# Prompt heads of a hybrid decoder: score banks, value tiles, mask and the second gelu rearranged

## The reference

```python
def trunk_layer(x, pos, conv_prev, h0, lp, paged=None):
    z = rms_norm(x, lp['attn_norm']) @ lp['w_in']      # split in xr, cq, ckv, kpe, u, v, g
    y_rg, h_last, conv_new = rglru_branch(xr, conv_prev, h0, pos, ...)   # softplus(-lam), convolution of 4 taps, scan
    q = (rms_norm(cq, lp['q_a_norm']) @ lp['w_uq']).reshape(bsz, t, MLA_HEADS, QK_HEAD)
    q_nope = rms_norm(q[..., :QK_NOPE], lp['q_nope_norm'])
    q_pe = rope(rms_norm(q[..., QK_NOPE:], lp['q_rope_norm']), pos)
    latent, k_pe = rms_norm(ckv, lp['kv_a_norm']), rope(rms_norm(kpe, lp['k_rope_norm']), pos)
    y_at = mla_prompt(...) if paged is None else mla_sample(...)
    y_cm, v_rows = sgu_branch(jax.nn.gelu(u), jax.nn.gelu(v), ...)
    proj = jnp.einsum('btnc,ncd->btnd', jnp.stack([y_rg, y_at, y_cm], axis=2), lp['w_branch'])
    x = x + jnp.sum(jax.nn.sigmoid(g) * proj, axis=2) @ lp['w_out']
    hf = rms_norm(x, lp['ffn_norm'])
    return x + (jax.nn.silu(hf @ lp['w_gate']) * (hf @ lp['w_up'])) @ lp['w_down'], ...

def attend(q_nope, q_pe, k_nope, k_pe, v, mask):
    s = (jnp.einsum('...qhd,...khd->...hqk', q_nope, k_nope)
         + jnp.einsum('...qhr,...kr->...hqk', q_pe, k_pe)) * ATTN_SCALE
    p = jax.nn.softmax(jnp.where(mask, s, NEG_INF), axis=-1)     # prompt: causal mask
    return jnp.einsum('...hqk,...khd->...qhd', p, v)

def sgu_branch(u, v_raw, ln_g, ln_b, w_s, b_s):                  # u and v_raw after gelu
    v = layer_norm(v_raw, ln_g, ln_b)
    w = jnp.where(tri, w_s, 0)                                   # 4 groups, chunks of 128 tokens
    s = jnp.einsum('gts,bcsgd->bctgd', w, vp) + b_s
    return u * s, v
```

## Time and profile before

| | us |
| --- | --- |
| median of 3 runs | 1579.79 (1579.55 to 1580.88) |
| profiled execution | 1578.23 |
| its span | 1576.3 |
| PE busy | 1550.4 (98%), 10796 matmuls |
| PEld busy | 1508.5 (96%) |
| DVE busy | 1073.9 (68%) |
| ACT busy | 891.8 (57%) |
| POOL busy | 531.2 (34%) |
| DMA | 142 GB/s; the main queue's packets take 44.5% of 16 engines' span |

### The profile page before, as it was taken

One profiled execution on the slowest core, in us unless ns is written; L12 is line 12 of the kernel. 1 busy time (PEld: TensorE's weight loads), 2 busy tenths in 40 slices (PEclk: granted clock), 3 DMA queues, 4 the chain that ended last, 5 costly groups with the idle time before them and its releaser, 6 DMA issues.

```text
span 1576.3 us, 33289 instructions
## 1 busy us (share of the span) xinstructions
PE 1550.4 (98%) x10796; PEld 1508.5 (96%) x10796; DVE 1073.9 (68%) x1620; ACT 891.8 (57%) x1740; POOL 531.2 (34%) x709
## 2 busy tenths in 40 slices
PE   8999999999999999999999999999999999999999
PEld 7988999999999999999999789999999999999999
DVE  6777778877674766664376877888775658666633
ACT  5787777677534444443357877777774335444422
POOL 4733377776700100000048223777766001000000
PEclk9999999999999999999999999999999999999999
DMA  7331454443644544444454224545436444444443
GB/s 278 121 102 51 120 174 145 142 146 104 192 138 149 149 147 149 155 149 147 147 189 129 79 67 118 178 140 154 140 112 186 144 150 148 147 147 150 154 147 114
DMA packets 114722, 224.65 MB, mean 143 GB/s; under 512 B 12881, under 2 KB 78706, under 8 KB 114482
## 3 DMA queue, kind: packets, MB, share of 16 engines
q1 hardware_dynamic: 112178, 214.75, 44.5%
q0 software_dynamic: 2432, 8.49, 1.6%
HBM read 220.73 MB, written 2.46 MB: 142 GB/s over the span
## 4 chain that ended last, share of the span: by engine, by line
PE 84%; DVE 6%; ACT 3%; DVEq 3%; issue 2%; ACTq 1%; DMA 0%; POOL 0%; SPq 0%; POOLq 0%
PE PS L847 54%; PE PS L1102 22%; DVE lt_lo L1800 1%; PE PS L1132 1%; DVEq L2078 1%; PE PS L1133 1%; DVE w_lo L1797 1%; DVE sraw L2077 1%; DVEq L1791 1%; ACT w_hi L1348 1%; PE PS L874 1%; PE PS L903 1%; PE PS L981 0%; ACTq L1535 0%; PE PS L1076 0%
## 5 line engine op out<-in xcount | busy, mean ns | idle before, releaser
L1797 DVE TENSOR_TENSOR w_lo<-raw,w_hi 128x1024 fp32r<-128x1024 f32 x258 | 326.0, 1265 | 219.4 <-ACT w_hi L1348 216.5
L1348 ACT ACTIVATE w_hi<-raw 128x1024 fp32r<-128x1024 f32 x258 | 272.2, 1057 | 347.4 <-PE PS L847 334.5
L847 PE MATMUL PS<-h_hi,w_hi 128*128 128x320 f32 x1360 | 426.4, 313 | 9.4 <-DVE h_lo L1824 8.7
L847 PE MATMUL PS<-h_hi,w_lo 128*128 128x320 f32 x1360 | 421.3, 310 | 0.0
L847 PE MATMUL PS<-h_lo,w_hi 128*128 128x320 f32 x1360 | 421.3, 310 | 0.0
L847 PEld LDWEIGHTS PS<-h_hi,w_hi 128*128 128x128 f32 x1360 | 256.4, 189 | 12.5 <-issue 7.8
L847 PEld LDWEIGHTS PS<-h_lo,w_hi 128*128 128x128 f32 x1360 | 256.4, 189 | 1.0
L847 PEld LDWEIGHTS PS<-h_hi,w_lo 128*128 128x128 f32 x1360 | 256.3, 188 | 0.0
L1102 PE MATMUL PS<-comb_hi,lt_hi 128*128 128x288 f32 x1024 | 224.2, 300 | 6.2 <-DVE lt_lo L1800 4.9
L1348 ACT ACTIVATE ksqp<-PS 128x512 f32<-128x512 f32 x256 | 152.4, 595 | 137.1 <-PE PS L1102 134.9
L1102 PE MATMUL PS<-comb_lo,lt_hi 128*128 128x288 f32 x1024 | 218.8, 295 | 0.0
(11 more groups left out here) (325 smaller groups left out, 2690.5 us busy)
## 6 DMA issues: line engine op xcount, KB each, us to landing
raw<-in_stream SPq DMA_DIRECT2D x258, 512.0 KB, 3.5
tpage<-in_tcache SPq DMA_DIRECT2D x256, 160.0 KB, 2.3
rrow<-in_rcache SPq DMA_DIRECT2D x256, 128.0 KB, 2.7
x<-in_xT SPq DMA_DIRECT2D x2, 640.0 KB, 5.5
sbias<-in_sbias POOLq DMA_DIRECT2D x2, 640.0 KB, 6.3
out_yT<-x SPq DMA_DIRECT2D x4, 320.0 KB, 2.2
const<-in_consts SPq DMA_DIRECT2D x1, 1090.0 KB
wgate<-in_wgate POOLq DMA_DIRECT2D x2, 512.0 KB, 4.9
```

What stands on the lines that cost most here:

```text
L847: done = mm(out, w[:, slot, c], a, start=first and n == 0 and m == 0, stop=last and n == len(pairs) - 1 and m == 2)
L1348: return nc.scalar.activation(out, in_, func, **kw)
L1797: V.tensor_tensor(w_lo[:, s, :], raw[:, s, :], f(w_hi[:, s, :]), ALU.subtract).then_inc(lo_done.sem, 1)
```

## The change

The scores get three banks (0, 1, 2), so they run three heads ahead. The transposes go to banks 3 and 5. A head's value tile becomes 128 wide, with zeros in the half that belongs to the pair's other head: both heads of a pair add up in one bank over all 128 partitions. The mask product covers the two diagonal blocks of 128 columns alone and comes last. The attention scale is folded into the gains of the queries, and the maxima come out negated, so L2012 goes. The new tokens' scores move behind the first two heads and the v transposes.

The second gelu's square and its product with the summed rows go to GpSimd; argument, sums, tanh and the last product run in halves. ScalarE loads the tanh table by an instruction of its own. `y2_hi` moves to pages 1 and 3 of the first sequence, `y2_lo` to pages 3 and 11. The DMAs of `hlast`, `convn` and `vrows` go from GpSimd's queue to SP's, as does the second load of `wv`. GpSimd runs the convolution ahead of softplus.

```diff
-PAIR_BANK = (4, 6, 7, 5)
+PAIR_BANK = (4, 6, 7, 6)
+PROB_BANK = (3, 5)
...
-    mask_r = sb("mask_r", [128, 384], f32r, on=under_wkT)
+    mask_r = sb("mask_r", [128, 128], f32r, on=under_wkT)
...
-    vp = sb("vp", [128, 2, H * DV], on=st3)
+    vp_first = sb("vp_first", [128, H * 128], on=st3)
@@ SP @@
+            sp.wait_ge(lru_h.sem, lru_h.at(l, 1))
+            sp.dma_start(outs["hlast"]...).then_inc(rows_sent.sem, 16)
+            sp.dma_start(outs["convn"]...).then_inc(rows_sent.sem, 16)
+            sp.wait_ge(vln.sem, vln.at(l, 1))
+            sp.dma_start(outs["vrows"]...).then_inc(rows_sent.sem, 16)
...
-            sp.wait_ge(sgu_y.sem, sgu_y.at(l, 2))
             sequence(l, 1)
             sp.wait_ge(p_free.sem, p_free.at(l, 1))
+            sp.dma_start(wv[:], ins["wv"]...).then_inc(wv_late.sem, 16)
             sequence(l, 2)
@@ POOL @@
-            softplus(l)
             for j in range(4):
                 pool.wait_ge(z_scaled.sem, z_scaled.at(l, 2 + j + 1))
...
+            softplus(l)
             pool.wait_ge(small_in.sem, small_in.at(l, 64))
...
+            nc.gpsimd.memset(by_half(vp_first)[:, :, 1:3], 0.0)
...
+            pool.wait_ge(var_mm.sem, var_mm.at(l, 1))
+            nc.gpsimd.tensor_tensor(ge[:], ua[:], ua[:], ALU.mult).then_inc(gsq.sem, 1)
+            new_scores_masked()
+            pool.drain()
+            other_sequences_masked()
+            for g in range(2):
+                part = slice(2 * g, 2 * g + 2)
+                pool.wait_ge(sgu_sum.sem, sgu_sum.at(l, g + 1))
+                nc.gpsimd.tensor_tensor(va[:, part], va[:, part], ua[:, part], ALU.mult).then_inc(sgu_p.sem, 1)
@@ PE @@
             def scores(h):
-                b = h % 2
+                b = h % 3
-                mm(PS[:, b, 0:384], ident_r[:], mask_r[:], start=True, stop=False)
-                for qt, c0, n in ((0, 0, 128), (1, 128, 256)):
+                for qt, c0, n in ((1, 128, 256), (0, 0, 128)):
...
+                diagonal = PS[:, b, 0:384].rearrange("p (n k) -> p n k", n=3)[:, 0::2]
+                mm(diagonal, ident_r[:], mask_r[:]....to_broadcast([128, 2, 128]), start=False, stop=True)
             def values(h):
-                o = PS[64 * (h % 2):64 * (h % 2) + 64, ob, :]
-                mm(o[:, 0:256], vp[:, 0, 64 * h:64 * h + 64], pT[:, h % 2, 0:256], start=True, stop=False)
-                mm(o[:, 128:256], vp[:, 1, 64 * h:64 * h + 64], pT[:, h % 2, 256:384], start=False, stop=True)
+                cols = slice(128 * h, 128 * h + 128)
+                mm(PS[:, ob, 0:256], vp[0][:, cols], pT[:, h % 2, 0:256], start=h % 2 == 0, stop=False)
+                mm(PS[:, ob, 128:256], vp[1][:, cols], pT[:, h % 2, 256:384], start=False, stop=h % 2 == 1)
...
             for h in range(H):
-                if h + 2 < H:
-                    scores(h + 2)
-                b = 2 + h % 2
+                if h + 3 < H:
+                    scores(h + 3)
+                b = PROB_BANK[h % 2]
@@ ACT @@
+            values_copied(0, 0)
             act.wait_ge(sgu_scaled.sem, sgu_scaled.at(l, 1))
...
             act.wait_ge(y0_ready.sem, y0_ready.at(l, 1))
+            values_copied(1, 7)
...
-            A(ge[:], ua[:], ACT.Square).then_inc(gsq.sem, 1)
+            exps(1)
             for h in range(H):
-                if h + 1 < H:
-                    exps(h + 1)
+                if h + 2 < H:
+                    exps(h + 2)
                 if h == 1:
-                    A(ge[:], ge[:], ACT.Tanh, scale=GELU_C).then_inc(gth.sem, 1)
+                    tanh_table()
+                    for g in range(2):
+                        spatial_tanh(l, g)
-                if h == 4:
-                    A(y2_hi[:], ge[:], ACT.Copy).then_inc(y2h.sem, 1)
...
+                if not tail and p in (1, 3):
+                    spatial_hi(l, p // 2)
@@ DVE @@
+            for g in (0, 2):
+                V.tensor_tensor(va[:, g:g + 2, :], PS[:, 4 + g:6 + g, 0:T], sbias[:, g:g + 2, :], ALU.add).then_inc(sgu_sum.sem, 1)
+                release(4 + g)
+                release(5 + g)
...
-                V.tensor_reduce(cols[:, 0:1], PS[:, h % 2, 0:128], AX.X, ALU.max)
-                V.tensor_reduce(cols[:, 1:2], PS[:, h % 2, 128:384], AX.X, ALU.max)
-                dve.drain()
-                V.tensor_scalar_mul(cols[:, 2:4], cols[:, 0:2], -SCALE).then_inc(ps_max.sem, 1)
+                V.tensor_reduce(cols[:, 0:1], PS[:, h % 3, 0:128], AX.X, ALU.max, negate=True)
+                V.tensor_reduce(cols[:, 1:2], PS[:, h % 3, 128:384], AX.X, ALU.max, negate=True).then_inc(ps_max.sem, 1)
```

More of the change, by code:

```diff
@@ L779, in sequence @@
                         rotary_lo(b + 1, 0)
-                    if c == 2 and isinstance(b, int) and b == 0:
-                        pool.wait_ge(y2_ready.sem, y2_ready.at(l, 1))
-                        pool.sem_inc(waits_passed, 1)
+                    first, second = (isinstance(b, int) and b == n for n in (0, 1))
+                    if c == 2 and first:
                         for i in range(RROWS):
@@ L786, in sequence @@
                         nc.gpsimd.memset(mx[HT:128], 0.0)
-                        pool.drain().then_inc(p_free.sem, 1)
+                        pool.drain()
+                    if c == 2 and second:
+                        pool.wait_ge(y2_ready.sem, y2_ready.at(l, 1))
+                        pool.sem_inc(p_free.sem, 1)
                     if values and c == 0:
@@ L1049, in prompt_attention @@
             v_transposed(l, 2, 7)
+            pe.wait_ge(bank_free[3].sem, banks.take(l, 3))
+            mm(PS[0:TS, 3, :], kpe[:, SEQ:T], qpz[:, :, SEQ:T], start=True, stop=False)
+            for j in range(4):
+                last = mm(PS[0:TS, 3, 128 * j:128 * j + 128], kT[:, j, SEQ:T], qz[:, 2 * j:2 * j + 2, SEQ:T],
+                          start=False, stop=j == 3)
+            last.then_inc(sn_mm.sem, 1)
             pe.wait_ge(vp_ready.sem, vp_ready.at(l, 2))
+            scores(2)
             for h in range(H):
-                if h + 2 < H:
-                    scores(h + 2)
-                b = 2 + h % 2
+                if h + 3 < H:
+                    scores(h + 3)
+                b = PROB_BANK[h % 2]
                 pe.wait_ge(ps_prob.sem, ps_prob.at(l, h + 1))
@@ L2138, in sequence @@
                 V.tensor_reduce(kss[:, par, p, :], ksqp[:, s, :].rearrange("p (h c) -> p h c", h=H), AX.X, ALU.add).then_inc(pk_ss.sem, 1)
[L2139 to L2144 removed]
+                if not tail and p == 3:
+                    spatial_lo(l, 0)
                 if not tail and p in (5, 9):
                     split(l, U_D + p // 4 - 1)
+                if not tail and p == 11:
+                    spatial_lo(l, 1).then_inc(y2_ready.sem, 1)
                 if not tail and p == 7:
```

220 lines of the change are left out of this document (112 added, 108 removed).

## The result

The changed kernel takes 1590.0 us at the median of five runs (1588.6 to 1592.1) against 1579.8 before: a ratio of 1.0066, 95% interval 1.0054 to 1.0077. The kernel is slower by 10.2 us where I forecast 2.2 faster, and lies outside my range. Its profiled execution took 1589.0 us, with a span of 1587.4, 11.1 more than before.

A forecast was written before the change was run, and what follows sets the result against it. TensorE (PE), busy 1550.4 of 1576.3 us, was taken as the bound. Per layer, -1.2 us in the prompt heads and +0.1 in the pages, twice, gave -2.2: 1577.6 us, range 1572.5 to 1581.8 for 8 in 10.

The forecast's parts named there:

- Convolution ahead of softplus: Stretch from 20 to 80 us: GpSimd's reordering costs 0, because PE is busy 60.0 of 60 us there.
- PE idle at the recurrence gates: Sign before the first page sequence: PE idle time there would show a part wrong that was costed at nothing.
- Bank 5 as the wait that the change adds: Prompt heads: PE's transposes of head 1 wait for VectorE's first bias sum, 2.2 us instead of 1.08.
- The square, and the turns: Prompt heads: GpSimd's square takes 3.0 us, each product 1.5; VectorE waits for whole GpSimd instructions, and they for its.
- My walk: Prompt heads, instruction by instruction with GpSimd's turns: bank 5 free at 121.3, stage end 135.5 instead of 136.67.
- the first rival: Prompt heads: port conflicts hardly matter, PE bounds the stage; -2.6 to -3.2 us per layer, about 1574.2; chance 0.28.
- PE work less by 1.1 us a layer: Prompt heads: narrower mask product saves 0.5 us, full-width value tiles 0.6; together 1.1, between 0 and 1.7.
- ScalarE as the chain from head 4 on: Prompt heads after 125.8: ScalarE's exponentials, copies and small waits make 9.0 us, to 134.8; last value product ends 135.5.
- this gap as a sign: Prompt heads: a gap on ScalarE before the exponential of head 4 would show the forecast right.
- The high parts of the gated rows: Pages 1 and 3, first sequence: 1.3 us of ScalarE work moved there, charged 0.1 a layer, between 0 and 1.3.
- The other moves at nothing: Output DMAs on SP, later value-weight load and zeroing of value tiles cost nothing: PE meets no wait where they stand.

## Why the prediction was wrong

**The step that failed** is "Convolution ahead of softplus: PE is busy 60.0 of the 60 us from 20 to 80, where both stand, so nothing waits for them, and it is 0." That PE never waits in a stretch shows only that nothing came too late there in the old order. It doesn't show by how much. Softplus ended at 47.0 and was first needed at 58.2: 11 us of slack. Moved behind the convolution it ended 14.8 us later, at 61.85. The way to see it was to follow the moved work's semaphore, `params`, to its one wait, on ScalarE ahead of the first gate tanh, and to set the two times side by side. I looked at what the convolution gains and never at what softplus loses. PE idle at the recurrence gates was what I had named as the sign that a zero was wrong, and it is the sign that came.

**A second part of the same step** had no term at all: a wait of PE is dearer than its length. The order cost 12.7 us in the profiled execution, for 7.8 us of idle time: 8.7 are the waits with what the matmuls lose in overlap, and 4.1 a lower clock behind them.

**Bank 5 as the wait that the change adds**: wrong. PE started the transposes of head 1 at 125.06, 0.17 us later than the work ahead of them would have let it. The first sum ran from 123.96 to 124.77, so bank 5 was free by then. My time for PE was nearly right (119.1 and the offset of 5.3 make 124.4), and mine for the sum was 1.8 us late (121.3 and 5.3 make 126.6).

**The square, and the turns.** I priced it at 3.0 us from a 512-column product with a converted output. It took 2.32 for 1280 columns; the two products took 1.55 each, as priced. The turns are there:

```profile
119.99 1.11 DVE L2067 TENSOR_SCALAR sp_<-sp_,pst 128x128 f32<-128x128 f32 x1
...
121.21 0.28 DVE L2059 TENSOR_REDUCE pst<-PS 128x1 f32<-128x128 f32 x1
121.41 0.41 DVE L2060 TENSOR_REDUCE pst<-PS 128x1 f32<-128x256 f32 x1
...
126.51 1.65 DVE L2068 TENSOR_SCALAR sp_<-sp_,pst 128x256 f32<-128x256 f32 x1
```

```profile
117.65 2.32 POOL L744 TENSOR_TENSOR ge<-ua 128x1280 f32<-128x1280 f32 x1
119.92 1.10 POOL L690 TENSOR_SCALAR_AFFINE_SELECT snew<-snew 64x512 f32<-64x512 f32 x1
121.21 1.09 POOL L694 TENSOR_SCALAR_AFFINE_SELECT snew<-snew 64x512 f32<-64x512 f32 x1 [0.19 <-issue]
...
124.95 3.05 POOL L752 TENSOR_TENSOR va<-va,ua 128x640 f32<-128x640 f32 x2 [2.65 <-DVE va L2035]
```

VectorE's multiplications took 1.11 where 0.29 is usual and 1.65 where 0.35 is, each until a GpSimd instruction had ended. That is the mechanism of the earlier trace rows again. The Trainium skill (SBUF — State Buffer, Who interferes with whom) has it as a lock held for a whole instruction, and these two rows agree. That reductions from PSUM are not held I had read from 109.26, where GpSimd ran nothing; the rows of 121.21 and 121.41 do show it, at their usual 0.28 and 0.41 beside a select. But the turns cost 2.1 us of VectorE's time in two places. My walk had 2.7 ahead of the bank's release alone (1.2 for the square's end, 1.5 for the selects) and the two products behind it, and the second turn ran while PE still had scores to do. So the first rival, "the ports hardly matter", had the better number for the heads, though the turns did come: it put the stage 2.6 to 3.2 us shorter, and it became 2.5 and 2.3 shorter.

**PE work less by 1.1 us a layer**: too small on PE (the wide tile alone takes 0.34 off each head's cycle, because the transposes ahead of it got cheaper too, 0.33 in place of 0.47) and too large in time won, where the tile was worth 0.22 in this stage.

**ScalarE as the chain from head 4 on**: half right. The chain went through VectorE to ScalarE:

```profile
129.32 0.37 ACT L1369 ACTIVATE sp_<-PS,pst 128x128 f32<-128x128 f32 x1 [2.64 <-DVE pst L2060]
```

I named this gap as a sign, and took it for given. Moving head 4's maxima ahead of head 3's normalisation and both heads' ahead of the page's split closed it, and gave 1.2 us a layer.

**The high parts of the gated rows**: I charged 0.1 with an upper end of 1.3, "if all of it came before a page split that PE waits for". They stood exactly there, and it was 0.66. The diff shows the place, right ahead of the next page's split; I should have taken the upper half.

**The other moves at nothing** (DMAs on SP, the later value weights, zeroing): no wait of PE is put down to them, but no run took them out either. The added 1.7 us in the later sequences of layer 2 had no term, its cause is open, and the moved DMAs may have a part in it.

With the order's cost left out the sum would have been right by luck, as errors of opposite sign cancel: 2.2 less forecast, 2.0 less measured, from heads at -2.4 a layer where I had -1.2, and pages at +0.65 a layer and +1.7 once, where I had 0.1 a layer.

## What to carry to other kernels

A moved piece of work has two ends: follow its semaphore to the first wait on it, read when that wait was met and when it was needed, and compare this slack with how far the end moves, also where the bottleneck engine shows no wait at all. Put a wait directly ahead of the first instruction that reads the result; one placed earlier makes everything queued behind it late. What a lighter instruction is worth depends on what bounds the stage, so the same tile was worth 0.2 us in one version and 0.75 in the next.

## What the runs showed of the hardware that was not expected

- A wait of TensorE of 1.53 us was followed by a granted clock of 0.91 over 20 us in one layer and of 1.00 in the other, in one execution, with the same busy time around it. In the run with the gelu parts back it fell after a wait of 1.48 us. Behind three waits of some 0.4 us each it fell at 794.9 us in the run with softplus first, and did not in the kernel before. After 4.8 us of waiting the clock was at its lower level for the next 5 us.
- Three 128-column transposes followed by a product into a tile 64 wide take 0.42 to 0.48 us to the product's start; with a tile 128 wide 0.33.
- GpSimd squared 1280 float32 columns in 2.32 us, 1.8 ns a column. Its products of two different tensors took 2.4 ns a column with float32 output (640 columns in 1.55 us) and 2.3 with converted output (512 in 1.20). So the output's type is not what made the square cheap.
- An idle time of TensorE of 3.04 us moved its later work by 3.6 us at full clock.
